# Triangular inverses of a two-block network on one core: cross-partition layout, four 64x64 tiles at once, one PSUM bank for each kind of product

## The chip, the cores and the metric

One Trainium2 chip, of which the kernel uses one core. The metric is the device time of one execution in microseconds (us), lower is better. The engines are named as in the profile: PE is TensorE (matmul), PEld its weight loads, DVE VectorE, ACT ScalarE, POOL GpSimd, SP the queue that issues DMAs.

## The reference, cut to what matters

The network has a first block (a convolution/LRU mixer and an mLSTM mixer, each with a feed-forward layer) and a second block, a layer with four mixers side by side and a gate for each. Sequence length 1024, width 1024, float32 throughout. Two of the four mixers are chunked delta rules: a gated delta net (in the kernel `gdn`, chunks of 64 in the reference) and an RWKV-7 style mixer (`rw`). Each has 4 heads of width 64. In the kernel a chunk is 128 positions, and each chunk of each head needs the inverse of a unit triangular 128x128 matrix, I + A with A strictly triangular, built from the keys. The inverses are what the change touches. There are 8 batches of 8 matrices: per mixer two pairs of heads by two halves of the sequence, and in a batch 2 heads by 4 chunks. The gates beside them are a dense product of the normed input with a wide weight:

```
mixed = gates[0] * (ys[0] @ w_branch[0])
for i in range(1, N_MIXERS):
    mixed = mixed + gates[i] * (ys[i] @ w_branch[i])
return x + mixed @ w_out
```

## The kernel before, in words

The whole network is one program. Five engine programs are written as Python generators; a `yield` ends a step. In the stretch that matters, `scans_tensor` and its twins for the other engines weave two streams step by step (`weave_beside`, L4315): `gdn` and then a sparse attention on one side, a spatial mixer and then `rwkv` on the other. Between the steps every engine takes steps of a third stream, the gates: dense float32r products of 128x128 by 128x512 (L476, `half_tensor`, three matmuls for a block), evicted by a multiply on DVE (L2775) and an activation on ACT (L2792). How many gate steps stand after which step is a hand-written table, `MORE_GATES` (L4311), the same for all engines. PE does its instructions in this order, so where it waits, the gates behind the wait stand too.

A batch of inverses (`Inverse`, L2944) holds, for 8 matrices e, A as [128, 8, 128], and 64-wide working arrays T, TC and X as [128, 8, 64]. The two diagonal 64x64 blocks of each matrix are inverted side by side, the upper one (TOP) in partitions 0 to 63, the lower one (BOTTOM) in 64 to 127. T is the inverse so far and TC its transpose. Each of five levels k = 1 to 5 has three kinds of product, each for 8 matrices and both blocks, so 16 matmuls of 64x64 by 64x64:

- x: A times T, masked by DVE into X (L3035);
- t: TC times X, subtracted from T by DVE (L3041);
- tt: X times TC, subtracted from TC by DVE (L3045; in the last level into TT, L3048).

`inverse_tensor` issues the x products as one step (one call of `product`) and t and tt together as the next (two calls). All of these matmuls are on line L2976. In what follows a block of x is the 16 matmuls of one step, a block of t/tt the 32 of the next. These operands are plain float32, and the trace has two MATMUL and two LDWEIGHTS records for each such matmul: a block of x has 32 records of each, a block of t/tt 64. A block p works with rows p (its operands lie in partitions p) and writes PSUM partitions p, so it uses the tile of the array at rows p and columns p: the matmuls of a block take turns between two tiles, rows TOP with columns TOP and rows BOTTOM with columns BOTTOM. `crossed` pairs TOP of one half of the matrices with BOTTOM of the other, and the halves of the matrices are in two PSUM banks, so the two tiles that run together write different banks. A bank of the t/tt step holds t in its first 256 columns and tt in its last 256.

Before the levels a "turn" (L2982, 16 matmuls against the identity) makes T from TC, copied by ACT (L3057). After them a sixth level (L2999, L3006, one tile each, 8 matmuls) joins the two diagonal blocks. Then the mixers use the inverse.

PSUM banks come from rings: `gdn` has banks 2, 3, 4 and `rwkv` banks 5, 6, 7. `take` (L297) makes PE wait until the bank's last user is read out.

Two other places of the same stretch matter for the prediction. L3450 in the spatial mixer and L3165 in `gdn` multiply 128 rows into 64 columns: L3165 eight records (four matmuls) into one column half, L3450 eight records into columns 0 to 63 and then eight into columns 64 to 127, with other weights and the same rows. L3986 in the attention is

```
for r in range(2):
    d = mm(K.ps[part(r, 64), b, 0:64], B.HK[64:128, :], B.W2[64:128, 0:64], start=True, stop=True, skip_group_check=True)
```

that is, two matmuls of 64x64 by 64x64 that both read partitions 64 to 127 and write PSUM partitions 0 to 63 and 64 to 127 of one bank.

Of the kernel before, what the change touches and what calls it, by code (L numbers as in the profile page):

```python
# [11 lines left out]
ACT = mybir.ActivationFunctionType  # L12
AX = mybir.AxisListType.X
MUL, ADD, SUB, MAX, MIN = ALU.mult, ALU.add, ALU.subtract, ALU.max, ALU.min

T = 1024
D = 1024
# [13 lines left out]
def part(n, w=128):  # L31
    return slice(n * w, n * w + w)


class Scope(ExitStack):
    def __init__(self, side="left"):
        super().__init__()
        self.side = side
# [29 lines left out]
class Seat:  # L68
# [20 lines left out]
    def after(self, K, name):  # L89

        for s in (K.T, K.V, K.S, K.G):
            self.wait_ge(*K.at(name, s))
# [16 lines left out]
class Ring:  # L109
# [6 lines left out]
    def take(self, user, hold=False):  # L116
        b, before = self.idle.popleft()
        self.of[user] = b
        if not hold:
            self.idle.append((b, user))  # L120
        return b, before
# [39 lines left out]
class Kernel:  # L161


    def __init__(self, nc, ctx):
        self.nc, self.ctx, self.names = nc, ctx, 0
        self.table, self.counting, self.signals = {}, True, []
        self.bank_of, self.rings, self.order, self.taken = {}, [], [], {}
        self.T, self.V, self.S, self.G = (self.semaphore(n) for n in ("tensor", "vector", "scalar", "gpsimd"))

# [70 lines left out]
class Split:  # L240
    def __init__(self, K, k, ctx):
        self.hi = K.sb([128, k, T], F32R, ctx, "xhi")
        self.lo = K.sb([128, k, T], F32R, ctx, "xlo")

# [9 lines left out]
class SplitApart(Split):  # L254


    def __init__(self, K, k, ctx, at):
        super().__init__(K, k, ctx)
        self.first = [K.sb_at(at + 4096 * i, [128, T], F32R, name="ysf") for i in range(2)]

# [610 lines left out]
def wait_steps(n):  # L871
    for _ in range(n):
        yield
# [2080 lines left out]
TOP, BOTTOM = part(0, 64), part(1, 64)  # L2954


def e8(x):
    return x.rearrange("p (a b) -> p a b", a=8)


def crossed():

    for h in range(2):
        for i in range(4):
            two = ((TOP, 4 * h + i), (BOTTOM, 4 * (1 - h) + i))
            yield from two if h == 0 else two[::-1]


def inverse_tensor(pe, K, Q, n, I):

    mm = pe.e.matmul

    def product(lhs, rhs, at, banks):
        for p, e in crossed():
            o = K.ps[p, banks[e // 4], part(4 * at + e % 4, 64)]
            d = mm(o, lhs[p, e, p] if lhs is I.A else lhs[p, e, :], rhs[p, e, :], start=True, stop=True, skip_group_check=True)  # L2976
        return d

    bs = [take(pe, K, Q, n, "turn", s) for s in range(2)]
    pe.wait_ge(*K.at(n, "tt", 0))  # L2980
    for p, e in crossed():
        d = mm(K.ps[p, bs[e // 4], part(e % 4, 64)], I.TC[p, e, :], K.ident[p, p], start=True, stop=True, skip_group_check=True)  # L2982
    d.then_inc(*K.T((n, "turned")))
    yield
    for k in range(1, 6):
        bs = [take(pe, K, Q, n, "x", k, s) for s in range(2)]
        pe.wait_ge(*K.at(n, "t", k - 1))
        product(I.A, I.T, 0, bs).then_inc(*K.T((n, "x mm", k)))
        yield
        bs = [take(pe, K, Q, n, "t", k, s) for s in range(2)]  # L2990
        pe.wait_ge(*K.at(n, "tt", k - 1))
        pe.wait_ge(*K.at(n, "x", k))
        product(I.TC, I.X, 0, bs)
        product(I.X, I.TC, 1, bs).then_inc(*K.T((n, "tt mm", k)))
        yield
    b = take(pe, K, Q, n, "x", 6)
    pe.wait_ge(*K.at(n, "t", 5))
    for e in range(8):
        d = mm(K.ps[BOTTOM, b, part(e, 64)], I.A[TOP, e, BOTTOM], I.T[TOP, e, :], start=True, stop=True, skip_group_check=True)  # L2999
    d.then_inc(*K.T((n, "x mm", 6)))  # L3000
    yield
    b = take(pe, K, Q, n, "tt", 6)
    pe.wait_ge(*K.at(n, "tt", 5))
    pe.wait_ge(*K.at(n, "x", 6))
    for e in range(8):
        d = mm(K.ps[TOP, b, part(e, 64)], I.X[BOTTOM, e, :], I.TT[BOTTOM, e, BOTTOM], start=True, stop=True, skip_group_check=True)  # L3006
    d.then_inc(*K.T((n, "tt mm", 6)))
    yield
# [6 lines left out]

def inverse_first(ve, K, H, n, I):

    for p in (TOP, BOTTOM):
        mask = H.level[0][p].unsqueeze(1).to_broadcast([64, 8, 64])
        ve.own().tensor_tensor(I.TC[p, :, :], I.A[p, :, p], mask, MUL).then_inc(*K.V())  # L3020
    ve.own().tensor_tensor(I.TC, H.ident64.unsqueeze(1).to_broadcast([128, 8, 64]), I.TC, SUB).then_inc(*K.V((n, "tt", 0)))


def inverse_half(K, n, name, k, s, at):
    return K.bank(n, name, k, s)[:, part(at, 256)].rearrange("p (a b) -> p a b", a=4)


def inverse_vector(ve, K, H, n, I):
    V = K.V
    yield  # L3030
    for k in range(1, 6):
        ve.wait_ge(*K.at(n, "x mm", k))
        mask = H.level[k].unsqueeze(1).to_broadcast([128, 4, 64])
        for s in range(2):
            ve.own().tensor_tensor(I.X[:, part(s, 4), :], inverse_half(K, n, "x", k, s, 0), mask, MUL).then_inc(*V((n, "x", k), ("free", (n, "x", k, s))))  # L3035
        yield
        rows = slice(0, 128) if k < 5 else TOP
        ve.wait_ge(*K.at(n, "tt mm", k))
        for s in range(2):
            T = I.T[rows, part(s, 4), :]  # L3040
            ve.own().tensor_tensor(T, T, inverse_half(K, n, "t", k, s, 0)[rows], SUB).then_inc(*V((n, "t", k)))  # L3041
        for s in range(2):
            tt, TC = inverse_half(K, n, "t", k, s, 1), I.TC[:, part(s, 4), :]
            if k < 5:
                ve.own().tensor_tensor(TC, TC, tt, SUB).then_inc(*V((n, "tt", k), ("free", (n, "t", k, s))))  # L3045
            else:
                for p in (TOP, BOTTOM):
                    ve.own().tensor_tensor(I.TT[p, part(s, 4), p], TC[p], tt[p], SUB).then_inc(*V((n, "tt", k), ("free", (n, "t", k, s))))  # L3048
        yield
    yield  # L3050
    yield


def inverse_scalar(se, K, n, I):
    se.wait_ge(*K.at(n, "turned"))
    for s in range(2):
        se.own().activation(I.T[:, part(s, 4), :], K.bank(n, "turn", s)[:, 0:256].rearrange("p (a b) -> p a b", a=4), ACT.Copy).then_inc(*K.S((n, "t", 0), ("free", (n, "turn", s))))  # L3057
    yield
    yield from wait_steps(10)
    se.wait_ge(*K.at(n, "x mm", 6))  # L3060
    se.own().activation(I.X[BOTTOM, :, :], e8(K.bank(n, "x", 6))[BOTTOM], ACT.Copy).then_inc(*K.S((n, "x", 6), ("free", (n, "x", 6))))
    yield
    se.wait_ge(*K.at(n, "tt mm", 6))
    se.own().activation(I.TT[TOP, :, BOTTOM], e8(K.bank(n, "tt", 6))[TOP], ACT.Copy, scale=-1.0).then_inc(*K.S((n, "inverse"), ("free", (n, "tt", 6))))
    yield
# [53 lines left out]
def gdn_tensor(pe, K, Q, H, B):  # L3119
# [31 lines left out]
    def body(j, q):  # L3151
        n = ("gdn", j, q)
        yield from inverse_tensor(pe, K, Q, (n, "inv"), B.inv)
        for s in range(2):
            p, hn = part(s, 64), (n, s)
# [44 lines left out]
def gdn_vector(ve, K, H, B):  # L3200
# [6 lines left out]
    def first(j, q, before):  # L3207
# [44 lines left out]
        yield  # L3252
        attention(n, 1)
        inverse_first(ve, K, H, (n, "inv"), B.inv)
        if q == 0:
            ve.own().memset(B.S[:, :], 0.0).then_inc(*V((n, "state", 0)))
# [39 lines left out]
def gdn_scalar(se, K, H, B):  # L3296
# [28 lines left out]
    def body(j, q):  # L3325
        n = ("gdn", j, q)
        turn_scalar(se, K, (n, "kg"), B.KG)
        turn_scalar(se, K, (n, "ko"), B.KO)
        yield from inverse_scalar(se, K, (n, "inv"), B.inv)
        for s in range(2):  # L3330
            p = part(s, 64)
            se.wait_ge(*K.at((n, s), "w mm"))
            se.own().activation(B.WT[p, :], K.bank((n, s), "w")[p, :], ACT.Copy).then_inc(*S(((n, s), "wt"), ("free", ((n, s), "w"))))
        yield
        for i in range(4):
            yield
            se.wait_ge(*K.at(n, "o mm", i))
            se.own().activation(B.O[:, part(i)], K.bank(n, "o", i)[:, 0:128], ACT.Copy).then_inc(*S((n, "o kept", i), ("free", (n, "o", i))))
            yield
# [199 lines left out]
def rwkv_tensor(pe, K, Q, H, B):  # L3539
# [43 lines left out]
    def body(j, q):  # L3583
        n = ("rw", j, q)
        yield from rounds(inverse_tensor(pe, K, Q, (n, "inv"), B.inv), reads(n))
        for s in range(2):
            p, hn = part(s, 64), (n, s)
# [51 lines left out]
def rwkv_vector(ve, K, H, B):  # L3639
# [8 lines left out]
    def first(j, q, before):  # L3648
# [53 lines left out]
        yield  # L3702
        ve.own().tensor_tensor(v4(B.R0), v4(RO), wide4(B.ECM), MUL).then_inc(*V((n, "r0")))
        inverse_first(ve, K, H, (n, "inv"), B.inv)
        yield
        for s in range(2):
# [1469 lines left out]
```

## Time and profile before

| | |
|---|---|
| median of 3 runs | 4079.07 us (4078.73 to 4081.39) |
| profiled execution, span | 4078.9 us |
| PE, PEld, DVE, ACT, POOL busy | 94%, 74%, 65%, 33%, 29% of the span |
| mean granted TensorE clock | 0.960 of full speed |
| first and last start on L2976 | 2868.6 and 3592.5 us |
| chain that ended last | PE 71%, DVE 22%, ACT 3% |

The span is that of the profiled execution and its own time; it stands 0.2 us from the median of the unprofiled runs. A granted clock of 1.00 is 2.4 GHz and 0.50 is 1.2 GHz. In a profile a row of the timeline merges neighbouring records of one line: its start, the time from the first start to the last end, the engine, the line and the number of records (x32). The end of a matmul record includes the way through the array, so the next block may start before the row's end.

### The profile page before, as it was taken

The page shows a single profiled execution, that of the slowest core. Times are in us where ns is not written, and L with a number is a line of the kernel's source. Part 1 is how long each engine was busy: PE and PEld are TensorE (multiplying, and loading weights), DVE is VectorE, ACT ScalarE, POOL GpSimd, SP SyncE. Part 2 cuts the span into 40 slices and gives each one's busy share as a digit, 9 for nine tenths or more (in the row PEclk, how much of TensorE's full clock was granted, in tenths as well). Part 3 has the DMA queues.
Part 4 walks back from the last instruction along what each step waited for, and adds up shares of the span by engine and source line. Part 5 has one row for each costly group of instructions (what it writes and reads, how often), then busy time and mean ns, then how long its engine had stood idle before and what let it go on. Part 6 is the DMA issues. An engine that isn't in the chain of part 4 may idle for free.

```text
span 4078.9 us, 51857 instructions
## 1 busy us (share of the span) xinstructions
PE 3830.4 (94%) x20718; PEld 3011.2 (74%) x20718; DVE 2658.7 (65%) x3054; ACT 1344.8 (33%) x1764; POOL 1193.2 (29%) x578
## 2 busy tenths in 40 slices
PE   8999999999889998999999989999999989999998
PEld 7567788877666766778887767887677767776777
DVE  7964878789865553487878888533545554546783
ACT  5242432244433333242324343212222131324512
POOL 2012044445213332114444422223122221212064
PEclk9999999999889999999999989999989989899999
DMA  3002232354311010223326332223211221323053
GB/s 112 21 26 84 106 108 93 110 181 149 121 68 37 32 37 26 93 98 116 101 92 209 129 133 101 94 104 117 83 56 54 74 78 63 116 75 106 28 205 145
DMA packets 131770, 385.58 MB, mean 95 GB/s; under 512 B 13565, under 2 KB 14209, under 8 KB 126281
## 3 DMA queue, kind: packets, MB, share of 16 engines
q1 hardware_dynamic: 131528, 382.27, 26.8%
q8 instruction: 163, 2.67, 0.3%
q14 instruction: 79, 0.64, 0.0%
HBM read 281.00 MB, written 101.22 MB: 94 GB/s over the span
## 4 chain that ended last, share of the span: by engine, by line
PE 71%; DVE 22%; ACT 3%; issue 2%; POOL 1%; DMA 1%; DVEq 0%; SPq 0%; ACTq 0%; POOLq 0%
PE ps L380 22%; PE ps L1453 21%; PE ps L476 8%; PE ps L2976 3%; PE ps L4489 2%; PE ps L907 2%; PE ps L2250 1%; DVE acc L1722 1%; PE ps L2242 1%; DVE top L1626 1%; DVE xop L1626 1%; PE ps L3077 1%; DVE x L661 1%; PE ps L4153 1%; DVE t L641 1%
## 5 line engine op out<-in xcount | busy, mean ns | idle before, releaser
L333 POOL TENSOR_TENSOR wlo<-wraw,whi 128x1024 fp32r<-128x1024 f32 x181 | 446.9, 2469 | 1772.4 <-ACT whi L325 1763.8
L1453 PE MATMUL ps<-xop,whi 128*128 128x512 f32 x1984 | 618.1, 393 | 14.3 <-DVE acc L1747 9.6
L325 ACT ACTIVATE whi<-wraw 128x1024 fp32r<-128x1024 f32 x185 | 196.1, 1060 | 921.3 <-PE ps L380 610.9
L1453 PE MATMUL ps<-top,whi 128*128 128x512 f32 x1488 | 468.3, 396 | 19.7 <-DVE acc L1716 15.9
L1453 PEld LDWEIGHTS ps<-xop,whi 128*128 128x128 f32 x1984 | 373.0, 188 | 99.3 <-DVE acc L1747 12.1
L1453 PE MATMUL ps<-xop,wlo 128*128 128x512 f32 x992 | 388.1, 391 | 0.0
L476 PE MATMUL ps<-xhalf,whi 128*128 128x512 f32 x1024 | 374.0, 448 | 0.3 <-POOL wlo L333 0.3
L1453 PEld LDWEIGHTS ps<-top,whi 128*128 128x128 f32 x1488 | 280.6, 189 | 87.6 <-DVE acc L1716 19.0
L1851 POOL TENSOR_TENSOR wlo<-wsum,whi 128x1024 fp32r<-128x1024 f32 (+2 forms) x102 | 229.1, 2246 | 362.7 <-ACT whi L1478 362.4
L380 PE MATMUL ps<-xhi,whi 128*128 128x512 f32 x868 | 307.0, 435 | 20.7 <-DVE xlo L681 9.1
L1453 PE MATMUL ps<-top,wlo 128*128 128x512 f32 x744 | 293.5, 394 | 0.0
L380 PE MATMUL ps<-xhalf,whi 128*128 128x512 f32 x1012 | 273.9, 393 | 11.0 <-DVE xhalf L681 8.6
L380 PE MATMUL ps<-xlo,whi 128*128 128x512 f32 x868 | 274.2, 397 | 0.0
L380 PE MATMUL ps<-xhi,wlo 128*128 128x512 f32 x868 | 272.2, 395 | 0.0
L1851 POOL TENSOR_TENSOR wlo<-wraw,whi 128x1024 fp32r<-128x1024 f32 (+2 forms) x80 | 183.2, 2290 | 244.7 <-ACT whi L1478 242.8
L380 PEld LDWEIGHTS ps<-xhalf,whi 128*128 128x128 f32 x1012 | 191.0, 189 | 53.6 <-DVE xhalf L681 11.2
L476 PEld LDWEIGHTS ps<-xhalf,whi 128*128 128x128 f32 x1024 | 180.9, 201 | 54.7 <-issue 25.0
L380 PEld LDWEIGHTS ps<-xhi,whi 128*128 128x128 f32 x868 | 160.9, 193 | 77.1 <-issue 27.8
L1453 PEld LDWEIGHTS ps<-xop,wlo 128*128 128x128 f32 x992 | 186.9, 188 | 41.2
L476 PE MATMUL ps<-xhalf,wlo 128*128 128x512 f32 x512 | 210.9, 412 | 0.0
L1478 ACT ACTIVATE whi<-wsum 128x1024 fp32r<-128x1024 f32 (+2 forms) x108 | 101.9, 943 | 298.3 <-PE ps L1453 125.1
L380 PEld LDWEIGHTS ps<-xlo,whi 128*128 128x128 f32 x868 | 166.4, 192 | 36.9
(637 smaller groups left out, 7132.8 us busy)
## 6 DMA issues: line engine op xcount, KB each, us to landing
wraw<-in_w_dram SPq DMA_DIRECT2D x185, 512.0 KB, 3.5
h_keep<-h SPq DMA_DIRECT2D x154, 256.0 KB, 4.5
wraw<-in_s_dram SPq DMA_DIRECT2D x48, 512.0 KB, 4.1
f<-h_keep SPq DMA_DIRECT2D x24, 768.0 KB, 5.5
wmore<-in_s_dram SPq DMA_DIRECT2D x32, 512.0 KB, 4.0
x_keep<-x SPq DMA_DIRECT2D x16, 1024.0 KB, 3.8
g_keep<-gates SPq DMA_DIRECT2D x64, 256.0 KB, 2.4
gb<-g_keep SPq DMA_DIRECT2D x32, 512.0 KB, 3.7
```

The source lines that it names most:

```text
L325: se.own().activation(K.hi(c), K.raw[:, c % NRAW, :], ACT.Copy).then_inc(*K.S(("hi", c)))
L333: ge.own().tensor_tensor(K.lo(c), K.raw[:, c % NRAW, :], K.hi(c).bitcast(F32), SUB).then_inc(*K.G(("lo", c)))
L380: done = pe.e.matmul(into[:, h, :], wt, x[h], start=(first and j == 0), stop=(last and j == 2), skip_group_check=True)
L476: done = mm(K.ps[:, b, :], wt, x, start=(i == 0 and j == 0), stop=(i == n - 1 and j == 2), skip_group_check=True)
L641: ve.own().tensor_tensor(acc, acc, sq, ADD).then_inc(*K.V((n, "add", i), (n, "add")))
L907: d = mm(K.ps[:, banks[h], :], M.diag[:, (BY_PE.index(j) * P_TAPS + k) % NDIAG, :], M.Yc[:, j, 512 * h + k:512 * h + k + 512], start=(k == ...
L1453: d = pe.e.matmul(out[:, s, :], w[:, o], x[:, i, :], start=(j < 3 and i == 0 and t == 0), stop=(i == k - 1 and t == 2), skip_group_check=True)
L1478: se.own().activation(F.whi(c), F.source(b, j), ACT.Copy).then_inc(*K.S((n, "whi", c)))
L1626: ve.own().tensor_tensor(F.olo[j][:, :k, :], source[:, :k, :], F.ohi[j][:, :k, :].bitcast(F32), SUB).then_inc(*K.V((F.name, "op", g, j)))
L1851: seat.own().tensor_tensor(F.wlo(c), F.source(b, j), F.whi(c).bitcast(F32), SUB).then_inc(*signal((F.name, "wlo", c)))
L2976: d = mm(o, lhs[p, e, p] if lhs is I.A else lhs[p, e, :], rhs[p, e, :], start=True, stop=True, skip_group_check=True)
L4489: done = mm(into, w, x, start=(i == 0 and j == 0), stop=(i == 7 and j == 2), skip_group_check=True)
```

## The change

The working arrays T and X move to the other 64 partitions in turn: TC of block p is kept in the opposite partitions o (`inverse_first` writes from p to o), the turn brings T back to p, the x products go from p to X in o, t goes from o to p, and tt stays in o. In terms of the array, turn, x and t use the two tiles whose rows and columns differ, tt the two tiles where they are the same. The t/tt step issues, for each matrix and each block, one matmul of t and one of tt in turn, so that four consecutive matmuls use all four 64x64 tiles. Each kind of product has one bank for all 8 matrices (512 columns), written from both row halves: turn, x, t and tt of a batch take one bank each, where turn, x and t/tt took two each. DVE and ACT read a whole bank in one instruction where they read two halves in two. The numbers of matmuls, of weight loads, of steps and of gate blocks between them stay, and so do the sixth level and all that follows. The helper `inverse_half` is gone.

```diff
+ACROSS = ((TOP, BOTTOM), (BOTTOM, TOP))
 def inverse_tensor(pe, K, Q, n, I):
-    def product(lhs, rhs, at, banks):
-        for p, e in crossed():
-            o = K.ps[p, banks[e // 4], part(4 * at + e % 4, 64)]
-            d = mm(o, lhs[p, e, p] if lhs is I.A else lhs[p, e, :], rhs[p, e, :], start=True, stop=True, skip_group_check=True)
+    def across(b, lhs, rhs):
+        for e in range(8):
+            for p, o in ACROSS:
+                d = mm(K.ps[o, b, part(e, 64)], lhs(p, e), rhs(p, e), start=True, stop=True, skip_group_check=True)
         return d
...
     for k in range(1, 6):
-        bs = [take(pe, K, Q, n, "x", k, s) for s in range(2)]
+        b = take(pe, K, Q, n, "x", k)
         pe.wait_ge(*K.at(n, "t", k - 1))
-        product(I.A, I.T, 0, bs).then_inc(*K.T((n, "x mm", k)))
-        yield
-        bs = [take(pe, K, Q, n, "t", k, s) for s in range(2)]
+        across(b, lambda p, e: I.A[p, e, p], lambda p, e: I.T[p, e, :]).then_inc(*K.T((n, "x mm", k)))
+        yield
+        bt, bc = (take(pe, K, Q, n, name, k) for name in ("t", "tt"))
         pe.wait_ge(*K.at(n, "tt", k - 1))
         pe.wait_ge(*K.at(n, "x", k))
-        product(I.TC, I.X, 0, bs)
-        product(I.X, I.TC, 1, bs).then_inc(*K.T((n, "tt mm", k)))
+        for e in range(8):
+            for p, o in ACROSS:
+                mm(K.ps[o, bt, part(e, 64)], I.TC[p, e, :], I.X[p, e, :], start=True, stop=True, skip_group_check=True)
+                d = mm(K.ps[p, bc, part(e, 64)], I.X[p, e, :], I.TC[p, e, :], start=True, stop=True, skip_group_check=True)
+        d.then_inc(*K.T((n, "tt mm", k)))
 def inverse_first(ve, K, H, n, I):
-    for p in (TOP, BOTTOM):
+    for p, o in ACROSS:
         mask = H.level[0][p].unsqueeze(1).to_broadcast([64, 8, 64])
-        ve.own().tensor_tensor(I.TC[p, :, :], I.A[p, :, p], mask, MUL).then_inc(*K.V())
+        ve.own().tensor_tensor(I.TC[o, :, :], I.A[p, :, p], mask, MUL).then_inc(*K.V())
 def inverse_vector(ve, K, H, n, I):
-        mask = H.level[k].unsqueeze(1).to_broadcast([128, 4, 64])
-        for s in range(2):
-            ve.own().tensor_tensor(I.X[:, part(s, 4), :], inverse_half(K, n, "x", k, s, 0), mask, MUL)...
+        mask = H.level[k].unsqueeze(1).to_broadcast([128, 8, 64])
+        ve.own().tensor_tensor(I.X, e8(K.bank(n, "x", k)), mask, MUL).then_inc(*V((n, "x", k), ("free", (n, "x", k))))
...
-        for s in range(2):
-            T = I.T[rows, part(s, 4), :]
-            ve.own().tensor_tensor(T, T, inverse_half(K, n, "t", k, s, 0)[rows], SUB).then_inc(*V((n, "t", k)))
+        ve.own().tensor_tensor(I.T[rows], I.T[rows], e8(K.bank(n, "t", k))[rows], SUB).then_inc(*V((n, "t", k), ("free", (n, "t", k))))
+        tt = e8(K.bank(n, "tt", k))
+        if k < 5:
+            ve.own().tensor_tensor(I.TC, I.TC, tt, SUB).then_inc(*V((n, "tt", k), ("free", (n, "tt", k))))
+        else:
+            for p, o in ACROSS:
+                ve.own().tensor_tensor(I.TT[p, :, p], I.TC[o], tt[o], SUB).then_inc(*V((n, "tt", k), ("free", (n, "tt", k))))
 def inverse_scalar(se, K, n, I):
-    for s in range(2):
-        se.own().activation(I.T[:, part(s, 4), :], K.bank(n, "turn", s)[:, 0:256].rearrange("p (a b) -> p a b", a=4), ACT.Copy)...
+    se.own().activation(I.T, e8(K.bank(n, "turn")), ACT.Copy).then_inc(*K.S((n, "t", 0), ("free", (n, "turn"))))
```

## Rows read from the trace of the kernel before

**Rows 1.** The page, span in 40 slices of 102 us: busy tenths, granted clock.
```profile
PE   8999999999889998999999989999999989999998
...
PEclk9999999999889999999999989999989989899999
```

**Rows 2.** Windows: width, busy PE, PEld, DVE, ACT, POOL; clock, DMA share, GB/s.
```profile
2858.00:3610.00 752.00, 707.24 (x7078) 557.90 (x7077) 380.94 (x715) 194.26 (x301) 148.38 (x64) 0.91 0.21 73
```

**Rows 3.** Groups by line, 2860 to 3600 us: busy us, mean ns, idle before <-releaser.
```profile
L476 PE MATMUL ps<-xhalf,whi 128*128 128x512 f32 x732 | 270.9, 453 | 0.0
...
L2976 PE MATMUL ps<-inv 64*64 64x64 f32 x3840 | 139.3, 230 | 0.2 <-DVE inv L3035 0.2
L2976 PEld LDWEIGHTS ps<-inv 64*64 64x64 f32 x3840 | 128.1, 144 | 31.2 <-issue 21.4 <-DVE inv L3045 3.3 <-DVE ps L2775 1.8
...
L3035 DVE TENSOR_TENSOR inv<-ps,c 128x256 f32<-128x256 f32 x80 | 34.0, 425 | 92.0 <-PE ps L2976 89.8
L3041 DVE TENSOR_TENSOR inv<-inv,ps 128x256 f32<-128x256 f32 (+1 forms) x80 | 33.5, 419 | 120.3 <-PE ps L2976 118.6
L2775 DVE TENSOR_TENSOR ps<-ps,t 128x512 f32<-128x512 f32 x46 | 32.2, 700 | 25.4 <-PE ps L476 23.5
```

**Rows 4.** Timeline, one level of one batch at full clock.
```profile
2888.14 1.15 PE L2976 MATMUL ps<-inv 64*64 64x64 f32 x32
...
2889.22 0.73 PE L476 MATMUL ps<-xhalf,whi 128*128 128x512 f32 x2
2889.35 0.88 DVE L3035 TENSOR_TENSOR inv<-ps,c 128x256 f32<-128x256 f32 x2 [1.56 <-PE ps L2976]
...
2890.81 2.08 PE L2976 MATMUL ps<-inv 64*64 64x64 f32 x64
...
2892.83 0.73 PE L476 MATMUL ps<-xhalf,whi 128*128 128x512 f32 x2
2892.95 0.88 DVE L3041 TENSOR_TENSOR inv<-inv,ps 128x256 f32<-128x256 f32 x2 [1.99 <-PE ps L2976]
...
2893.86 0.88 DVE L3045 TENSOR_TENSOR inv<-inv,ps 128x256 f32<-128x256 f32 x2
...
2895.09 1.01 PEld L2976 LDWEIGHTS ps<-inv 64*64 64x64 f32 x32 [0.35 <-DVE inv L3045]
```

**Rows 5.** Timeline, the sixth level: one tile only.
```profile
2918.77 1.14 PE L2999 MATMUL ps<-inv 64*64 64x64 f32 x16
```

**Rows 6.** Timeline of L3986, the 30 ns from 3576.270 us.
```profile
3576.28 0.27 PE L3986 MATMUL ps<-n 64*64 64x64 f32 x2
...
3576.28 0.14 PEld L3986 LDWEIGHTS ps<-n 64*64 64x64 f32 x2
```

**Rows 7.** Timeline, 128 rows into 64 columns: one column half, then both.
```profile
2932.40 1.09 PE L3165 MATMUL ps<-inv,g 128*64 128x128 f32 x8
```
```profile
2863.68 1.58 PE L3450 MATMUL ps<-sgw,sg 128*64 128x128 f32 x16
```

**Rows 8.** Windows of L3450 alone; counts include records in flight.
```profile
2863.67:2864.16 0.49, 0.49 (x5) 0.49 (x5) 1.00 0.83 306
2864.16:2864.66 0.49, 0.49 (x11) 0.49 (x10) 1.00 0.97 360
```

**Rows 9.** Timeline and window of a t/tt block at half clock, and what followed.
```profile
3194.49 3.68 PE L2976 MATMUL ps<-inv 64*64 64x64 f32 x64
...
3198.22 0.88 DVE L3041 TENSOR_TENSOR inv<-inv,ps 128x256 f32<-128x256 f32 x2 [6.74 <-PE ps L2976]
...
3204.96 0.69 DVE L3250 TENSOR_TENSOR inv<-ps,g 128x512 f32<-128x512 f32 x1
3205.70 0.96 PEld L3077 LDWEIGHTS ps<-g 64*128 64x128 f32 x8 [2.41 <-DVE inv L3250]
```
```profile
3194.50:3198.00 3.50, 3.50 (x65) 3.48 (x64) 0.00 (x0) 1.06 (x1) 2.22 (x1) 0.50 0.00 0
```

More of the change, by code:

```diff
@@ L2958, in e8 @@
     return x.rearrange("p (a b) -> p a b", a=8)
[L2961 to L2966, printed above, removed]
+ACROSS = ((TOP, BOTTOM), (BOTTOM, TOP))
 def inverse_tensor(pe, K, Q, n, I):
     mm = pe.e.matmul
-    def product(lhs, rhs, at, banks):
-        for p, e in crossed():
-            o = K.ps[p, banks[e // 4], part(4 * at + e % 4, 64)]
-            d = mm(o, lhs[p, e, p] if lhs is I.A else lhs[p, e, :], rhs[p, e, :], start=True, stop=True, skip_group_check=True)
+    def across(b, lhs, rhs):
+        for e in range(8):
+            for p, o in ACROSS:
+                d = mm(K.ps[o, b, part(e, 64)], lhs(p, e), rhs(p, e), start=True, stop=True, skip_group_check=True)
         return d
-    bs = [take(pe, K, Q, n, "turn", s) for s in range(2)]
+    b = take(pe, K, Q, n, "turn")
     pe.wait_ge(*K.at(n, "tt", 0))
-    for p, e in crossed():
-        d = mm(K.ps[p, bs[e // 4], part(e % 4, 64)], I.TC[p, e, :], K.ident[p, p], start=True, stop=True, skip_group_check=True)
-    d.then_inc(*K.T((n, "turned")))
+    across(b, lambda p, e: I.TC[p, e, :], lambda p, e: K.ident[p, p]).then_inc(*K.T((n, "turned")))
     yield
     for k in range(1, 6):
-        bs = [take(pe, K, Q, n, "x", k, s) for s in range(2)]
+        b = take(pe, K, Q, n, "x", k)
         pe.wait_ge(*K.at(n, "t", k - 1))
-        product(I.A, I.T, 0, bs).then_inc(*K.T((n, "x mm", k)))
+        across(b, lambda p, e: I.A[p, e, p], lambda p, e: I.T[p, e, :]).then_inc(*K.T((n, "x mm", k)))
         yield
-        bs = [take(pe, K, Q, n, "t", k, s) for s in range(2)]
+        bt, bc = (take(pe, K, Q, n, name, k) for name in ("t", "tt"))
         pe.wait_ge(*K.at(n, "tt", k - 1))
         pe.wait_ge(*K.at(n, "x", k))
-        product(I.TC, I.X, 0, bs)
-        product(I.X, I.TC, 1, bs).then_inc(*K.T((n, "tt mm", k)))
+        for e in range(8):
[3 more added lines that the diff above has]
+        d.then_inc(*K.T((n, "tt mm", k)))
         yield
@@ L3016, in inverse_first @@
 def inverse_first(ve, K, H, n, I):
-    for p in (TOP, BOTTOM):
+    for p, o in ACROSS:
         mask = H.level[0][p].unsqueeze(1).to_broadcast([64, 8, 64])
-        ve.own().tensor_tensor(I.TC[p, :, :], I.A[p, :, p], mask, MUL).then_inc(*K.V())
+        ve.own().tensor_tensor(I.TC[o, :, :], I.A[p, :, p], mask, MUL).then_inc(*K.V())
     ve.own().tensor_tensor(I.TC, H.ident64.unsqueeze(1).to_broadcast([128, 8, 64]), I.TC, SUB).then_inc(*K.V((n, "tt", 0)))
-def inverse_half(K, n, name, k, s, at):
-    return K.bank(n, name, k, s)[:, part(at, 256)].rearrange("p (a b) -> p a b", a=4)
 def inverse_vector(ve, K, H, n, I):
@@ L3032, in inverse_vector @@
         ve.wait_ge(*K.at(n, "x mm", k))
-        mask = H.level[k].unsqueeze(1).to_broadcast([128, 4, 64])
-        for s in range(2):
-            ve.own().tensor_tensor(I.X[:, part(s, 4), :], inverse_half(K, n, "x", k, s, 0), mask, MUL).then_inc(*V((n, "x", k), ("free", (n, "x", k, s))))
+        mask = H.level[k].unsqueeze(1).to_broadcast([128, 8, 64])
+        ve.own().tensor_tensor(I.X, e8(K.bank(n, "x", k)), mask, MUL).then_inc(*V((n, "x", k), ("free", (n, "x", k))))
         yield
@@ L3038, in inverse_vector @@
         ve.wait_ge(*K.at(n, "tt mm", k))
-        for s in range(2):
-            T = I.T[rows, part(s, 4), :]
-            ve.own().tensor_tensor(T, T, inverse_half(K, n, "t", k, s, 0)[rows], SUB).then_inc(*V((n, "t", k)))
-        for s in range(2):
[L3043 to L3048, printed above, removed]
+        ve.own().tensor_tensor(I.T[rows], I.T[rows], e8(K.bank(n, "t", k))[rows], SUB).then_inc(*V((n, "t", k), ("free", (n, "t", k))))
[5 more added lines that the diff above has]
+                ve.own().tensor_tensor(I.TT[p, :, p], I.TC[o], tt[o], SUB).then_inc(*V((n, "tt", k), ("free", (n, "tt", k))))
         yield
@@ L3055, in inverse_scalar @@
     se.wait_ge(*K.at(n, "turned"))
-    for s in range(2):
-        se.own().activation(I.T[:, part(s, 4), :], K.bank(n, "turn", s)[:, 0:256].rearrange("p (a b) -> p a b", a=4), ACT.Copy).then_inc(*K.S((n, "t", 0), ("free", (n, "turn", s))))
+    se.own().activation(I.T, e8(K.bank(n, "turn")), ACT.Copy).then_inc(*K.S((n, "t", 0), ("free", (n, "turn"))))
     yield
```

## The prediction

> **What bounds the kernel now.** I read the page's slices first: PE is 80 to 90% busy or more in every slice, and its clock dips most in slices 29 to 36 [rows 1]. That is the stretch of the inverses, and one window over it says what sets the time there: of 752 us PE works 707 and DVE 381, at a mean clock of 0.91 [rows 2]. So 45 us of this stretch are gaps of PE, the rest is matmuls one behind the other. PE takes its instructions in a fixed order and fills the waits of the inverses with gate blocks, so a matmul that gets shorter brings the end nearer as long as the next thing PE asks for is ready by then.
>
> The groups by line show what PE does there: gate products and, second, the 3840 records of L2976, 139.3 us [rows 3]. Its idle time before them is 21.4 us of "issue", 54 times some 0.4 us, which is PE emptying the array before the small tiles begin, and 3.3 us that end with DVE's L3045. DVE on the other hand waits for L2976 nearly each time: 90 us before L3035 and 119 us before L3041. In this pair PE is the one that is waited for.
>
> One level on the timeline makes it plain [rows 4]: the x block takes 2889.22 - 2888.14 = 1.08 us of PE, two gate blocks and the switch 1.59 us, the t/tt block 2892.83 - 2890.81 = 2.02 us, three gate blocks and the switch 2.26 us. Meanwhile DVE needs 0.88 us after x and 0.88 for T, then 0.88 for TC. It is done before PE comes back each time.
>
> **Part 1: the t/tt block with four tiles.** 16 matmuls of 64x64 on one tile have a row of 1.14 us for 16 records (8 matmuls) [rows 5]; the x block has 1.15 us for 32 records [rows 4]. The second tile is therefore free: each tile needs some 58 ns for a record ((1.14 - 0.27)/15, with 0.27 us for the last record), whatever the other does. The 64 records of t/tt on two tiles take 2.08 us, as 32 per tile must. On four tiles it is 16 per tile: 1.15 us, plus the start of two more tiles, 7 ns or so each, say 1.17. What is not in that row is whether two tiles that share rows and differ in columns run together, which the kernel before never asks of L2976. Other lines do. L3986 issues two such matmuls, and within 30 ns both loads and both first matmuls have begun [rows 6]. L3450 has 16 records in 1.58 us where one column half takes 1.09 us for 8 [rows 7], so 2 x 1.09 in series would be 2.0; its count of records in flight doubles, from 5 to 11 per half microsecond, as soon as the second column half joins [rows 8]. There the two tiles have different weights and the same rows, at twice the rows of these tiles, so reading the operands is no new load. I take full overlap.
>
> Saved per block at full clock: 2.08 - 1.17 = 0.91 us. There are 8 batches x 5 levels = 40 such blocks. Some fall into half clock and take 3.68 us instead of 2.08, clock 0.50 [rows 9]; they save more. The whole of L2976 is 139.3 us [rows 3], against 40 x (1.15 + 2.08) = 129.2 at full clock, a factor of 1.078. Saved: 40 x 0.91 x 1.078 = 39.2 us.
>
> **Part 2: the x and turn blocks.** Same numbers of matmuls, again on two tiles that differ in rows and columns; only the columns are crossed. I cost them at nothing. Both tiles now write one bank, in different partitions, which no row of before shows; see the third rival.
>
> **Part 3: DVE and ACT.** Two reads of 128x256, 0.88 us together [rows 4], become one of 128x512, which on L2775 takes 0.70 and on L3250 0.69 [rows 3, 9]. There are 5 x + 5 t + 4 tt pairs and two pairs in the last level for each batch, 16 x 8 = 128 pairs, by 0.18 us: 23 us of DVE. Inside the levels DVE's work is hidden behind PE's gate blocks, so this saves nothing directly. It saves a little where PE waits for a DVE queue that holds inverse work. The case is in [rows 9]: after the t/tt block DVE does TC, a gate, two operations of gdn, X and two more of gdn, and PE waits 1.97 us for L3250. In that gap three pairs become shorter, 0.5 us; there are some 4 to 6 gaps of the kind among the 45 us. I take 2 us. The writes from one half of the partitions into the other (`inverse_first`, the last TT) are not in the trace; as long as they cost an ordinary operation they are nothing, and were they twice as long, 32 x 0.69 = 22 us of DVE, they would be hidden by the same gates but for the same few gaps, 2 us lost.
>
> **Part 4: banks.** Before, the x block of the next level waited for the bank that L3045 frees, 1.3 us after the t/tt block; now it needs T alone, 0.7 us after. PE fills 2.26 us there, so nothing on the path. With one bank per kind a level takes three banks of the ring of three, each last used by something that the block must wait for anyway, so no new wait. In `rwkv` the products of `reads` take a bank in between; DVE reads them before T, so that holds too.
>
> **Does the saving reach the end?** In [rows 9] DVE stood idle for 6.74 us until the t/tt block was through, and the gap that follows hangs on that block. So the chain through the gap begins at L2976 and moves with it. The other gaps follow bursts of DVE work that stand in program order behind such a row; DVE is busy only 381 of 752 us [rows 2], so it does not carry a backlog from one level to the next, and I take nothing off for them. What comes after 3610 us is unchanged and only begins earlier.
>
> **Sum.** 39.2 + 2 = 41 us off the span of 4078.9; the runs' median of 4079.07 is the same within 0.2 us. Forecast 4038 us, 1.0% faster. Less than 0.2% (8 us) is about what a measurement of this kernel could not tell from no change.
>
> **The clock.** A mean of 0.91 over 752 us is 0.09 x 752 x 2 = 135 us at 0.50 [rows 2]. I keep its share as it is. If it grew or shrank by an eighth, 16 us at half clock, the time would move by 8 us.
>
> **Rivals.**
>
> - *Partly together, chance 0.14.* PE looks only so far ahead. In L3450 the second column half starts not with the first but after five of its eight records [rows 8]: three records or some six instructions wait at once. Four tiles ask for up to two records waiting in three tiles, just that many. If it is one less, the fourth tile of a group starts late; worked through with that rhythm the block takes 1.4 to 1.6 us and saves 0.5 to 0.6, so 40 x 0.55 x 1.078 + 2 = 26 us: 4053, within 4048 to 4060. The Trainium skill (TensorEngine Tiling (Array Packing), Instruction Overhead) gives each matmul some 60 cycles of overhead; if all tiles had to share that, it would be 25 ns x 64 = 1.6 us a block, an estimate from that page, and about 4059. The two matmul records of rows 6 that start within 30 ns speak against it, though only for one pair.
> - *Issue is the limit, nothing gained, chance 0.07.* 128 instructions in 2.02 us, 15.8 ns each, is the fastest sustained rate I found in the trace [rows 4]. If that is PE's own rate and not the tiles', four tiles bring nothing, and only part 3 is left: 4077. Against it: one tile runs at half that rate and two tiles at exactly twice, with no sign of bending [rows 4, 5].
> - *One bank cannot be written from two row halves at once, chance 0.06; the slower side.* The blocks of x and turn then run as if on one tile, 0.93 us longer each, 48 blocks: 48 x 0.93 x 1.078 = 48 us lost; in t/tt the two tiles of t exclude each other and so do those of tt, so 32 records follow each other for each kind and nothing is gained: 4079 + 48 - 2 = 4125 us. It decides from the first x block on: 2.0 us instead of 1.08. Before, `crossed` kept the banks of the two row halves apart, so no row can show it. The Trainium skill says just this (TensorEngine Tiling (Array Packing), Gotcha 1: PSUM Pressure): tiles of different rows cannot access one bank simultaneously; no run here shows it. It puts the duty on the software, with no stall, so I give the slowdown little.
> - *More half clock, chance 0.07.* The gaps stay and the work between them shrinks, so the clock may fall more often: 25 us or more of the 41 lost, 4063 and above, at worst no gain.
>
> **Chances and range.** Forecast 0.66, own range 4026 to 4048. Faster by more than 0.2%: forecast, partial and most of the clock case, 0.86. Within 0.2%: the issue limit, 0.07. Slower: the bank and a bad clock, 0.07. The range for 8 in 10 takes the forecast, the partial case and the near end of the clock case: 4023 to 4066; its low end is the forecast with the clock's 8 us and the DVE gaps' full worth, 7 us.
>
> **What would show it.** Right: rows of L2976 with x64 of 1.17 us, x32 still 1.15; PE busy on L2976 down from 139 to about 100; one DVE row of 0.70 for each kind; the last start of L2976 near 3552; the mean clock of the stretch near 0.91. Wrong: x64 at 1.4 or more (look-ahead), at 2.1 (issue), x32 at 2.1 (bank), or the blocks as forecast with a clock under 0.88. The prediction falls if an x32 block gets longer at all, for there are as many of these as of the others.

## The result, and the profile after

In the first series the changed kernel took 4020.92 us (median of 4 runs, 4012.28 to 4023.64) against 4078.9 of the kernel before; the ratio is 0.9857, with a 95% interval of 0.9834 to 0.9879. The forecast was 4038 with a range from 4023: the direction is right, the time lies 2 us below the range. Over all series of the study the medians are 4018.6 us (13 runs) and 4076.0 us (52 runs), 57 us apart where 41 were forecast.

Single runs of one kernel differ (the kernel before: 4051.6 to 4090.6 us, the changed one: 4010.4 to 4027.5), so I split each run in two. The span times the mean granted clock is the work at full clock; what is left of the span is what the half clock costs ("clock loss"; it also counts half-clock time in which PE stood idle, 14 to 18 us of the loss in every profiled run). Each run lists both factors. Means with their standard errors:

| kernel | runs | median us | work at full clock | clock loss |
|---|---|---|---|---|
| before | 52 | 4076.0 | 3913.3 +- 0.5 | 159.6 +- 1.1 |
| changed | 13 | 4018.6 | 3869.8 +- 0.8 | 147.1 +- 1.5 |

So 43.5 us are work and 12.5 us are the clock. At full clock the forecast was 40 x 0.91 + 2 = 38.4 us of work; the rest of its sum, 2.8 us, was the clock's share in the blocks.

The profiled execution of the changed kernel (4012.28 us, span 4010.5, the fastest of its series). The page's slices first, then the stretch of the inverses as a window (the columns of [rows 2]), first to its end and then over the same 752 us as before:

```profile
PE   8999899999889999999999998999999989998998
...
PEclk9999999999989999999999998999999989999999
```

```profile
2858.00:3533.50 675.50, 638.17 (x7021) 493.61 (x7019) 350.96 (x582) 187.68 (x286) 146.43 (x63) 0.94 0.24 80
2858.00:3610.00 752.00, 711.30 (x7414) 552.44 (x7413) 384.23 (x653) 205.77 (x311) 163.68 (x71) 0.94 0.25 83
```

The stretch now ends at 3533.5 us, where it ended at 3600.7: 67 of the 68 us between the two spans. The last block starts at 3525.3 us, where 3552 was forecast. PE's gaps are 675.5 - 638.2 = 37 us. The clock is at 0.94 where [rows 2] has 0.91.

The groups by line, 2860 to 3560 us (x and turn are L2971, t L2988, tt L2989; DVE's reads of x, t, tt L3026, L3030, L3033):

```profile
L2989 PE MATMUL ps<-inv 64*64 64x64 f32 x1280 | 50.0, 232 | 0.0
L2988 PE MATMUL ps<-inv 64*64 64x64 f32 x1280 | 50.0, 232 | 0.0
L2971 PE MATMUL ps<-inv 64*64 64x64 f32 x1280 | 48.3, 228 | 0.0
...
L3026 DVE TENSOR_TENSOR inv<-ps,c 128x512 f32<-128x512 f32 x40 | 27.6, 691 | 96.8 <-PE ps L2971 96.4
L3030 DVE TENSOR_TENSOR inv<-inv,ps 128x512 f32<-128x512 f32 (+1 forms) x40 | 27.4, 686 | 80.3 <-PE ps L2989 80.0
L3033 DVE TENSOR_TENSOR inv<-inv,ps 128x512 f32<-128x512 f32 x32 | 22.0, 687 | 1.1
```

Each group has its own busy time, and t and tt run at once: the two rows of 50.0 us are the same 50 us. With x they are 98 us, against 139.3 on L2976 [rows 3]. The 1280 + 1280 + 1280 records are the same 3840.

One t/tt block and the x block after it, on the timeline; the first line is of the kernel before, the gate record just ahead of the t/tt block in [rows 4]:

```profile
2890.49 0.40 PE L476 MATMUL ps<-xhalf,wlo 128*128 128x512 f32 x1
```
```profile
2882.06 0.39 PE L476 MATMUL ps<-xhalf,wlo 128*128 128x512 f32 x1
...
2882.37 0.27 PE L2988 MATMUL ps<-inv 64*64 64x64 f32 x1
2882.38 0.27 PE L2989 MATMUL ps<-inv 64*64 64x64 f32 x1
2882.39 0.27 PE L2988 MATMUL ps<-inv 64*64 64x64 f32 x1
2882.39 0.27 PE L2989 MATMUL ps<-inv 64*64 64x64 f32 x1
...
2883.32 0.22 PE L2989 MATMUL ps<-inv 64*64 64x64 f32 x1
2883.46 0.74 PE L476 MATMUL ps<-xhalf,whi 128*128 128x512 f32 x2
...
2884.32 0.69 DVE L3033 TENSOR_TENSOR inv<-inv,ps 128x512 f32<-128x512 f32 x1
...
2885.76 1.15 PE L2971 MATMUL ps<-inv 64*64 64x64 f32 x32
...
2886.96 0.69 DVE L3026 TENSOR_TENSOR inv<-ps,c 128x512 f32<-128x512 f32 x1 [1.94 <-PE ps L2971]
```

Four matmuls, one for each tile, begin within 20 ns. The 64 records start within 2883.32 - 2882.37 = 0.95 us, and with the 0.22 us of the last one the row would be the 1.17 us of the forecast. From the start of the last gate record before the block to the start of the first after it ("gate to gate") are 2883.46 - 2882.06 = 1.40 us; in the kernel before it is 2892.83 - 2890.49 = 2.34. That is 0.94 us less where 0.91 was forecast, and it is the measure by which the variants below are compared. The x block has its 1.15 us as before.

### The profile page after: what moved, and what is told of

Same layout as the page of the kernel before. It is cut to its first block, busy times and chain, and to the rows that moved or that the text cites. A ratio compares the mean times of both kernels' runs of the same rounds, so it can differ in the third digit from the quotient of the medians.

```text
span 4010.5 us, 51700 instructions
## 1 busy us (share of the span) xinstructions
PE 3772.6 (94%) x20718; PEld 2957.9 (74%) x20718; DVE 2630.1 (66%) x2926; ACT 1343.8 (34%) x1756; POOL 1193.1 (30%) x578
## 4 chain that ended last, share of the span: by engine, by line
PE 71%; DVE 22%; ACT 4%; issue 1%; POOL 1%; DMA 1%; DVEq 0%; SPq 0%; ACTq 0%; POOLq 0%
PE ps L380 22%; PE ps L1453 21%; PE ps L476 9%; PE ps L4476 2%; PE ps L907 2%; PE ps L2250 1%; PE ps L2971 1%; DVE top L1626 1%; DVE acc L1722 1%; PE ps L2242 1%; DVE xop L1626 1%; PE ps L3064 1%; DVE x L661 1%; PE ps L2988 1%; DVE t L641 1%
```

## The experiments

All variants keep numbers and order of everything outside the inverses, unless said.

**The two parts, each undone.** First the changed kernel once more, as base.

> The changed kernel once more, as the base for the three beside it and for its own spread. Prediction's miss: the t/tt blocks gave what was forecast (41.8 us by the trace) and some 15 to 25 us more came from the clock and the gaps. Theory 'clock is chance' expects a median that wanders by 10 us or more between series; theory 'the clock follows from the change' expects 4012 to 4024 us again, with 82 to 100 us at half clock in the stretch of the inverses.

4017.05 us (4013.92 to 4020.82), work 3871.8, clock loss 143.6 +- 1.0. It repeats: nothing wanders by 10 us from one series to the next, as the first theory had it.

Two tiles only:

```diff
-                mm(K.ps[o, bt, part(e, 64)], I.TC[p, e, :], I.X[p, e, :], ...)
-                d = mm(K.ps[p, bc, part(e, 64)], I.X[p, e, :], I.TC[p, e, :], ...)
+                mm(K.ps[o, bt, part(e, 64)], I.TC[p, e, :], I.X[p, e, :], ...)
+        for e in range(8):
+            for p, o in ACROSS:
+                d = mm(K.ps[p, bc, part(e, 64)], I.X[p, e, :], I.TC[p, e, :], ...)
```

> The changed kernel with all 16 matmuls of t issued before all 16 of tt: layout, banks, whole-bank reads and numbers stay, but only two tiles ever run together. The x64 block should be 2.08 us again, so 40 x 0.92 = 37 us more at full clock. Theory 'PE time alone' (clock and gaps have other causes): 4058 to 4062 us. Theory 'short blocks also keep the clock up': the half-clock time goes back from 85 towards 133 us as well and the time to 4070 to 4080. If the four tiles gave nothing: 4021.

4055.55 us (7 runs, 4049.28 to 4064.42), ratio to before 0.9959 (0.994 to 0.9978). Work 3897.7 +- 2.1: 26 to 28 us above the changed kernel, less than the 37 expected. The timeline says why:

```profile
2882.83 0.40 PE L476 MATMUL ps<-xhalf,wlo 128*128 128x512 f32 x1
...
2883.16 0.97 PE L2988 MATMUL ps<-inv 64*64 64x64 f32 x26
2883.92 0.27 PE L2991 MATMUL ps<-inv 64*64 64x64 f32 x2
...
2884.09 0.98 PE L2991 MATMUL ps<-inv 64*64 64x64 f32 x27
2885.00 0.73 PE L476 MATMUL ps<-xhalf,whi 128*128 128x512 f32 x2
```

Gate to gate is 2.17 us, not 2.34. In the crossed layout tt (here L2991) needs the two tiles that t leaves alone, and its first records start at 2883.92, while t still runs: 0.17 us per block, 7 us in all, come from the layout even without interleaving. With 2.17 - 1.40 = 0.77 us for 40 blocks 31 us were to be lost; 26 to 28 were. The clock loss is 157.0 +- 3.7, 13 us above the base beside it and 10 above the mean of the changed kernel. So part of the clock's gain seems to go with the four tiles, but the variant with both parts undone, below, has 5 us less loss than this one, and the means of one kernel's series differ by up to 7 us.

Half reads (DVE and ACT read 256 columns at a time, as before):

```diff
+        for s in range(2):
+            ve.own().tensor_tensor(I.X[:, part(s, 4), :], inverse_half(K, n, "x", k, s), mask, MUL)...
-        ve.own().tensor_tensor(I.X, e8(K.bank(n, "x", k)), mask, MUL)...
```

> The changed kernel, but DVE and ACT read each bank in two instructions of 256 columns, as before the change; four tiles stay. DVE gets 23 us more work. Theory 'whole-bank reads only shorten a few gaps': 2 to 7 us more, 4023 to 4028, gaps of PE back from 36 to about 43 us. Theory 'they are the missing 17 us, by fewer gaps and so a better clock': 4035 to 4040, half-clock time over 110 us. Theory 'hidden entirely': 4021.

4027.8 us (6 runs, 4016.46 to 4043.08), ratio 0.9887 (0.9865 to 0.9908). Work 3875.9 +- 1.4, clock loss 150.3 +- 3.8. The window over its inverses, and the same of the changed kernel from its first turn on:

```profile
2857.60:3547.20 689.60, 646.78 (x7013) 500.95 (x7014) 372.55 (x707) 189.01 (x294) 145.59 (x63) 0.93 0.23 78
```
```profile
2860.30:3533.50 673.20, 637.06 (x7014) 492.96 (x7014) 348.85 (x579) 187.68 (x286) 146.43 (x63) 0.94 0.24 80
```

PE's gaps are 42.8 us with half reads and 36.1 with whole ones: the whole reads shorten gaps, by 7 us in this pair of profiles and by 4 to 6 us of work in the means. The first theory holds, above the 2 us that I had put into the sum. The medians lie 11 us apart; the 7 us beyond the work are clock loss, with an error of 4 us.

Both undone. (This is also the test of the bank rival: of the change only the crossed layout and the bank for each kind are left.)

> Both: two tiles only and half reads, so that of the change only the crossed layout and the bank for each kind is left. If layout and banks are worth nothing this is the kernel before: 4075 to 4080 us. If two row halves writing one bank cost anything, above 4080. If the earlier release of T and the banks shorten gaps, 4065 to 4072. The difference to the run with two tiles only is the worth of whole-bank reads without four tiles.

4057.13 us (12 runs, 4051.88 to 4069.0), ratio 0.996 (0.9945 to 0.9974), work 3905.1 +- 1.0, clock loss 151.8 +- 1.9. Work is 8.2 us below the kernel before: the 7 us of t and tt overlapping at their seam, and what is left, 1 us, for all else in layout and banks. Two row halves writing different partitions of one bank cost nothing. Against the variant with two tiles and whole reads the work is 7.4 us more and the gaps of one profile 43 us for 35, but the medians are only 2 us apart, since the clock loss fell by 5 us.

**How far PE looks past a busy tile.** The t/tt block with two matmuls of a tile in a row, and with four:

```diff
-        for e in range(8):
-            for p, o in ACROSS:
+        for e0 in range(0, 8, 2):          
+            for p, o in ACROSS:
+                for e in range(e0, e0 + 2):
                     mm(K.ps[o, bt, ...
+                for e in range(e0, e0 + 2):
                     d = mm(K.ps[p, bc, ...
```

> The changed kernel with two matmuls of a tile in a row (four records) before the next tile's: A A B B C C D D in place of A B C D, same work and waits. It asks how far PE looks past a busy tile. Theory 'one shared look-ahead of about six instructions' (the prediction's partial case): the x64 row grows from 1.16 to about 1.9 us, total about 4021 + 31. Theory 'a queue of about six for each tile': about 1.3 us, total about 4026.

4040.22 us (2 runs; too few to judge the total), work 3872.8 +- 4.5, clock loss 165.6 +- 8.2. The trace decides: gate to gate

```profile
2879.91 0.40 PE L476 MATMUL ps<-xhalf,wlo 128*128 128x512 f32 x1
...
2881.47 0.72 PE L476 MATMUL ps<-xhalf,whi 128*128 128x512 f32 x2
```

is 1.56 us, 0.16 above four tiles in turn, near the 0.14 of a queue for each tile; a shared look-ahead of six instructions would have made it some 2.1.

> As the run with groups of two, with groups of four matmuls (eight records) of a tile in a row. Either look-ahead is then too short to keep four tiles busy: x64 row of 2.3 to 2.5 us, longer than the 2.08 of two tiles that alternate, and 4021 + 45 to 60 us in all. A row near 1.2 us would say that PE looks much farther ahead than both.

4091.11 us (one run), work 3929.8, 60 us more than the changed kernel's. Gate to gate:

```profile
2875.37 0.40 PE L476 MATMUL ps<-xhalf,wlo 128*128 128x512 f32 x1
...
2878.31 0.74 PE L476 MATMUL ps<-xhalf,whi 128*128 128x512 f32 x2
```

2.94 us, more than was expected and slower than the old order's 2.34. The same 64 records on the same four tiles take from 1.40 to 2.94 us by their order alone.

These figures can be worked through. Take 58 ns for a record on its tile (from [rows 5]), records given out in program order, and a tile that holds one record at work and two waiting (six instructions with their loads); when the tile of the next record is full, all behind it stand. That gives 0.17, 0.75 and 1.57 us more than four tiles in turn for two matmuls in a row, for two tiles and then the other two, and for four in a row; measured are 0.16, 0.77 and 1.54. With one record waiting it would be 1.04, 0.81 and 1.97, with three 0, 0.70 and 1.16. It is a model that fits three figures, not a thing that the trace shows.

**What the clock follows.** Does PE time on few tiles bring the clock down? Each x block issued twice, and each t/tt block issued twice:

> The changed kernel with each x block issued twice (the same products into the same bank), so 40 blocks of 0.93 us more, on two tiles, with the gaps and the rest as they are. Theory 'PE time alone': 37 to 40 us more, 4058 to 4061. Theory 'thinly used stretches bring the clock down': half-clock time up from 85 to 110 to 135 us, 4070 to 4080.

4048.86 us (4 runs, 4043.24 to 4055.11), work 3906.6 +- 0.9 (37 more), clock loss 140.6 +- 2.0: no more than the changed kernel's.

> The changed kernel with each t/tt block issued twice on four tiles: the same PE time more as with x twice, 40 x 0.93 = 37 us, but with twice the matmuls in it. PE time alone: 4058 to 4061, as x twice. If it is the fullness of the array that keeps the clock up, this one stays near 4058 while x twice is slower by 10 us or more; if both are alike, the kind of work in the block does not matter to the clock.

4062.6 us (6 runs, 4057.15 to 4068.53), work 3907.8 +- 1.3 (38 more), clock loss 153.0 +- 2.1. Both give the work that was expected, and the clock goes the wrong way for the theory: of the two, timed side by side, the one with 37 us more on two tiles loses 12 us less than the one with the same time more on four. Against the changed kernel, which was not timed beside them, both lie about as far off as its own series differ. The theory asked for 12 to 25 us more loss with x twice; that thinly used blocks as such bring the clock down so far is refuted.

**Gates to where PE waits.** In the changed kernel T is ready earlier after t/tt, so one of three gate blocks there can go. A new table `MORE_GATES` takes these 36 and puts 41 in front of 17 places where the trace has gaps (at three places one is taken and put back, so the tables differ by 33 against 38; the five more are gates that otherwise come later).

```diff
-MORE_GATES = {1: 12, 18: 3, 27: 1, 31: 1, 35: 1, 39: 1, 43: 3, 47: 5, 66: 1, ...
+MORE_GATES = {1: 12, 18: 3, 41: 3, 43: 3, 47: 5, 53: 4, 74: 1, 88: 2, 111: 5, 115: 5, 123: 1, 125: 5, 142: 1, 152: 2, 158: 2, ...
```

> The changed kernel with another table of gate steps: the 36 single extra gates that stand after the t/tt blocks (PE needs two gates there now, not three, since T is ready 0.9 us after the block) go to the 17 places where PE stood idle, 41 gates in all, each gap of the trace filled by its length over 0.69 us. The computation and its order within each stream stay. Theory 'gaps bring the clock down': gaps fall from 36 to under 12 us and the half-clock time in the stretch from about 85 to under 40 us: 3960 to 3975 us. Theory 'the clock has other causes': only the gaps go, 3990 to 3997. If the levels then wait for DVE: 4010 or more.

4009.64 us (6 runs, 4004.32 to 4012.81), ratio 0.9845 (0.9818 to 0.9873). Work 3866.3 +- 0.9, clock loss 140.9 +- 2.0. It is clearly faster than the kernel before. By the medians it is 9 us faster than the changed kernel, but that one was timed in other series, and its ratios of 0.9857, 0.986 and 0.9867 lie in this one's interval, so this is not shown. Neither theory's figure came. The time is near that of the third case, but not for its reason: in this profile the blocks of the levels wait only 1.2 us for DVE. The gaps are still there, elsewhere.

```profile
2858.90:3531.20 672.30, 637.00 (x7028) 495.62 (x7029) 351.67 (x579) 188.28 (x287) 145.91 (x63) 0.94 0.24 81
```
```profile
3450.26 1.61 PE L3064 MATMUL ps<-r 64*128 64x128 f32 x13
3455.23 1.64 PE L3064 MATMUL ps<-r 64*128 64x128 f32 x6 [3.35 <-DVE r L3679]
```

35 us of gaps. In the changed kernel this place waited 2.56 us ahead of L2941, which feeds DVE's L3679, and 1.87 us at L3064; here L2941 does not wait, and L3064 waits 3.35 within one step. At this place the gap is the end of a chain through DVE, and the fill only moved it along.

> The kernel before with the same new table and nothing else. If the saving of the table is independent of the change: as many us faster than before as the other is than the changed kernel (25 to 55). If the old bank order matters (the x block of the next level waits for the read of TC's first half, 1.3 us after t/tt, and two gates and the switch give 1.6), no stall either; with a busy DVE some 36 x 0.2 us are lost, 5 to 10 us less gained.

4050.32 us (11 runs, 4046.22 to 4059.24), ratio 0.9944 (0.9928 to 0.996), work 3900.4 +- 1.2, clock loss 149.5 +- 1.6. The same table gives the old inverses 26 us, 13 of work and 10 of clock. The table and the change overlap: of the table's 13 us of work only 3.5 are left on top of the change. The gaps say why. From the first turn to the end of the inverses, the kernel before and this one:

```profile
2860.70:3600.70 740.00, 696.45 (x7014) 548.95 (x7014) 374.86 (x707) 188.92 (x294) 145.99 (x63) 0.91 0.21 73
```
```profile
2860.80:3577.30 716.50, 681.92 (x7029) 540.75 (x7029) 368.61 (x707) 189.64 (x295) 146.38 (x63) 0.93 0.23 76
```

With half reads the table takes PE's gaps from 43.6 to 34.6 us. The whole reads alone take them to 36, and with both they are 35: the two ways shorten the same gaps, and some 35 us stay under either.

> A second try at the table of gate steps, from the gaps that the first try left: the longest of them (2.1 to 3.4 us) lie at or inside one step of the rwkv stream whose two groups of products both wait for DVE, so the fill now stands ahead of that step; the long stretches of gates after the sixth level give some up. The inverses are those of the changed kernel. Theory 'the gaps were filled at the wrong side of the step': gaps from 35 to under 20 us, half clock from 75 to under 60: 3985 to 3995 us. Theory 'the waits are a chain that the fill itself delays': gaps stay over 30 us and only change their places: 4005 to 4015.

4016.57 us (4 runs, 4010.86 to 4018.01), work 3870.2 +- 2.3, clock loss 143.5 +- 3.5; no better than the changed kernel beside it. The gaps are 33 us (671.5 wide, PE busy 638.1). The second theory holds, its time missed by 2 us: what is left of the gaps does not go by filling.

> The changed kernel once more on the chip and in the series of the run beside it, to compare them and to see how much of the clock part repeats: 4014 to 4022 us, work at full clock (span times mean clock) 3870 to 3873, clock loss (span less that) 140 to 148 us, against 158 to 163 of the kernel before.

4018.35 us (5 runs, 4010.41 to 4027.48), work 3867.3 +- 0.9, clock loss 150.3 +- 2.8. The total repeats within 4 us over three series. Work was expected at 3870 to 3873 and lies 3 us below, the clock loss at 140 to 148 and lies above; its three means are 146.6, 143.6 and 150.3.

## Why the prediction was too small

**What bounds the kernel.** Right. PE in its fixed order set the time of the stretch, and time taken from it reached the end whole: 40 x 0.94 = 38 us of blocks at full clock, 43.5 us of work in the means.

**Part 1.** Right: full overlap of the four tiles, 0.94 us a block for 0.91. The rows that carried it, L3986 and L3450 [rows 6 to 8], were enough, and the rivals "partly together" and "issue is the limit" fell with the timeline of one block: four starts within 20 ns, all 64 within 0.95 us. The look-ahead of the first rival is there, but for each tile, so that one matmul for each tile in turn never meets it. The 60 cycles for each matmul that the Trainium skill names (TensorEngine Tiling (Array Packing), Instruction Overhead) do not add up across tiles here: 64 records in 0.95 us are 15 ns each, below the 25 ns of the estimate.

**Part 2 and the bank rival.** The x blocks kept 1.15 us with both row halves in one bank, and the variant with nothing but layout and banks left was 8 us of work faster, not slower. The rule that the Trainium skill states (TensorEngine Tiling (Array Packing), Gotcha 1: PSUM Pressure) does not show as a delay here: the x blocks kept their 1.15 us. The two row halves always write different partitions of the bank; no run has them write the same ones.

**Part 3.** The mechanism is right, the size was short: 2 us in the sum, 4 us (half against whole reads on four tiles) to 7 us (on two tiles) measured. I counted three shorter pairs in one gap and four to six such gaps; the profiles show gaps of 43 us shrinking to 36.

**Part 4.** Right: nothing to speak of, 1 us.

**The clock: the step that failed.** The step is "I keep its share as it is", with 8 us either way. The loss fell from 159.6 to 147.1 us, 12.5 us in the mean where 2.8 were in the sum. Of the 16 us by which the saving was too small (57 for 41) 10 are this term; 5 are work, most of it part 3. With the work as measured and the clock's term as I had it, the forecast would have been 4079 - 43.5 - 2.8 = 4033 us, inside the range.

The 8 us either way were too narrow as well. Ahead of 2858 us every variant runs the same program, and in the fourteen profiles the half clock costs from 77 to 96 us there. That is scatter and not the change. In the two profiles of before and after this part is alike (82 us both), and the stretch of the inverses has 133 us at half clock before and 85 after; the other two profiles of the changed kernel have 79 and 75. The 24 us of loss in that pair are twice what the means of all runs show, so I go by the means. Two windows of the same place, the step with L3138 (before) and L3125 (after), show what differs: first the kernel before,

```profile
3180.00:3184.60 4.60, 4.60 (x23) 2.34 (x19) 3.95 (x8) 0.61 (x2) 0.10 (x1) 1.00 0.43 150
3184.60:3198.20 13.60, 13.60 (x127) 11.42 (x125) 5.98 (x9) 1.06 (x1) 4.08 (x2) 0.50 0.19 71
```

then the changed one:

```profile
3146.00:3150.00 4.00, 4.00 (x31) 2.13 (x22) 3.38 (x5) 1.57 (x3) 0.00 (x0) 1.00 0.58 197
3150.00:3153.40 3.40, 3.40 (x37) 2.58 (x36) 2.79 (x4) 0.00 (x0) 1.79 (x1) 0.50 0.53 194
```

The clock falls just after the same work, but stays down for 13.6 us in one and 3.4 us in the other. At the longest gap, 4.09 us in both, both stay at half clock for 10.2 us, first before, then after:

```profile
3123.10:3133.30 10.20, 6.54 (x21) 4.74 (x22) 7.68 (x13) 0.49 (x2) 0.00 (x0) 0.50 0.23 77
```
```profile
3092.00:3102.20 10.20, 6.46 (x21) 4.65 (x22) 7.65 (x14) 0.58 (x2) 0.00 (x0) 0.50 0.23 77
```

My rival "more half clock" had the wrong sign: I argued that the gaps stay while the work between them shrinks, and did not ask what else could change. What it is that helps stays open. It is not the fullness of the blocks (x twice and t/tt twice). With layout and banks alone the loss is 8 us lower than before, with whole reads added to them 3 us, with four tiles added instead 9 us, and with another gate table alone and the old inverses 10 us. These do not add up to a term for each part; that the loss reacts to where gaps and blocks fall in time is my reading and not shown. No variant isolates one cause, and the means of a single kernel's series differ by up to 7 us.

Together: 38 for the blocks at full clock, 4 to 7 for whole reads, 1 for the rest and 12.5 for the clock make 55 to 59 us; 57 were measured.

## What to carry to other kernels

Small matmuls cost next to nothing on tiles that would be idle, also on tiles that share their rows (0.94 us less for a block of 64 records), as long as consecutive matmuls change the tile; two in a row cost 0.16 us a block, and four in a row made the same block twice as long. The evidence for such an overlap stands in the trace of the kernel before, at lines other than the changed ones. And where the granted clock costs 160 us of a run, put its reaction into the range with the spread that runs and profiles of one kernel show (single runs of the kernel before lose from 142 us, span 4063.3 at a clock of 0.965, to 176 us, 4087.3 at 0.957, as span times the missing share), not with a share kept constant.

## What the runs showed of the hardware

- The order in which a block visits the tiles decides: gate to gate 1.40 us (one matmul for each tile in turn), 1.56 (two), 2.17 (two tiles, then the other two), 2.34 (two tiles), 2.94 (four in a row). The values fit, within 0.03 us, one record at work and two waiting for each tile, given out in program order, and not one look-ahead shared by all (a model, not seen as such).
- Two tiles that differ in rows write different partitions of one bank at no cost: the x block has 1.15 us with one bank as with two.
- One kernel's time scatters by where the half clock falls: 77 to 96 us of loss in the same first 2858 us. The work at full clock repeats far better (3913.4, 3912.6, 3913.5 and 3913.2 in four series of the kernel before).
- Filling a wait of PE with other work shortened the kernel before by 26 us (gaps from 44 to 35 us), the changed one by 9 us or less (36 to 35): some 35 us of gaps stay. The one followed up is the end of a chain through DVE.
